# First layer of the compression MLP in decode: two products per half, or three over pairs of blocks

## What is computed

```
idx = arange(nc)[:, None] * 16 + arange(32)[None, :]
blk = rows[:, idx] + pos_emb          # blocks of 32 rows, one every 16 rows
hidden = gelu(blk @ w1)               # w1: (32 * 64) x 128
out = hidden @ w2                     # 128 x 64
```

## Time and profile before

| | us |
|---|---|
| median of 3 runs (lowest, highest) | 1865.72 (1865.47, 1865.9) |
| the profiled execution: its time | 1868.04 |
| the profiled execution: its span | 1866.3 |
| TensorE busy in the span | 1838.7 (99%) |
| TensorE weight loads | 1412.1 (76%) |
| VectorE busy | 1204.6 (65%) |
| ScalarE busy | 372.3 (20%) |
| GpSimd busy | 119.1 (6%) |
| mean granted TensorE clock | 0.998 |
| DMA | 199.86 MB, mean 107 GB/s |

### The profile page before, as it was taken

One profiled execution on the slowest core, in us unless ns is written; L12 is line 12 of the kernel. 1 busy time (PEld: TensorE's weight loads), 2 busy tenths in 40 slices (PEclk: granted clock), 3 DMA queues, 4 the chain that ended last, 5 costly groups with the idle time before them and its releaser, 6 DMA issues.

```text
span 1866.3 us, 27349 instructions
## 1 busy us (share of the span) xinstructions
PE 1838.7 (99%) x10438; PEld 1412.1 (76%) x10438; DVE 1204.6 (65%) x2676; ACT 372.3 (20%) x957; POOL 119.1 (6%) x218
## 2 busy tenths in 40 slices
PE   8999999999999999999999999999999999999999
PEld 7767777877777777777777676777777777777777
DVE  5899796442667677673268997954427667676631
ACT  2013375322100100000001134842211000100000
POOL 1011400110000000000000114001000000000000
PEclk9999999999999999999999999999999999999999
DMA  7302564663112222131242044057431212222111
GB/s 276 129 1 88 161 209 157 214 221 111 57 68 72 87 68 90 58 136 63 80 152 79 1 122 143 1 182 249 161 122 45 90 69 80 78 70 109 72 62 51
DMA packets 110390, 199.86 MB, mean 107 GB/s; under 512 B 13393, under 2 KB 81250, under 8 KB 105266
## 3 DMA queue, kind: packets, MB, share of 16 engines
q1 hardware_dynamic: 90946, 161.87, 25.5%
q0 software_dynamic: 5488, 29.93, 4.6%
q10 hardware_dynamic: 13824, 6.30, 1.3%
HBM read 190.36 MB, written 15.94 MB: 111 GB/s over the span
## 4 chain that ended last, share of the span: by engine, by line
PE 94%; DVE 4%; ACT 1%; issue 1%; DMA 0%; POOL 0%; DVEq 0%
PE ps L1065 30%; PE ps L1130 15%; PE ps L755 12%; PE ps L616 8%; PE ps L651 8%; PE ps L603 7%; PE ps L859 2%; PE ps L822 2%; PE ps L841 2%; PE ps L999 1%; PE ps L659 1%; PE ps L893 1%; PE ps L908 1%; PE ps L695 1%; PE ps L862 1%
## 5 line engine op out<-in xcount | busy, mean ns | idle before, releaser
L2140 DVE TENSOR_TENSOR xT<-xT,ps 128x288 f32<-128x288 f32 (+3 forms) x55 | 41.7, 758 | 153.2 <-PE ps L1130 152.9
L1065 PE MATMUL ps<-catT,rD 128*128 128x288 f32 x528 | 131.6, 406 | 0.0
L1065 PEld LDWEIGHTS ps<-catT,rD 128*128 128x128 f32 x528 | 100.3, 190 | 27.7
L1497 ACT ACTIVATE rD<-rD 128x592 f32<-128x592 f32 x44 | 30.7, 697 | 450.2 <-DVE rD L2082 450.2
L755 PE MATMUL ps<-WR,rD 128*128 128x254 f32 (+1 forms) x512 | 120.2, 382 | 0.2
L1065 PE MATMUL ps<-catT,XC 128*128 128x288 f32 x480 | 119.8, 406 | 0.4 <-DVE rD L2054 0.4
L1065 PE MATMUL ps<-rA,WR 128*128 128x288 f32 x448 | 117.8, 406 | 0.0
L1065 PEld LDWEIGHTS ps<-catT,XC 128*128 128x128 f32 x480 | 91.0, 190 | 26.2 <-issue 1.2
L755 PEld LDWEIGHTS ps<-WR,rD 128*128 128x128 f32 x512 | 93.0, 188 | 18.6 <-issue 2.9
L1065 PEld LDWEIGHTS ps<-rA,WR 128*128 128x128 f32 x448 | 85.1, 190 | 23.5
L616 PE MATMUL ps<-catT,WR 128*128 128x288 f32 x384 | 98.8, 410 | 2.0 <-ACT catT L1231 1.1
(11 more groups left out here) (376 smaller groups left out, 3317.7 us busy)
## 6 DMA issues: line engine op xcount, KB each, us to landing
WR<-in_w_up SPq DMA_DIRECT2D x56, 512.0 KB, 3.7
WR<-in_kvc SPq DMA_DIRECT2D x128, 128.0 KB, 2.3
rB<-in_w_up SPq DMA_DIRECT2D x32, 512.0 KB, 4.3
rD<-in_kvc SPq DMA_DIRECT2D x96, 128.0 KB
rD<-in_w_down SPq DMA_DIRECT2D x8, 1408.0 KB, 7.6
rB<-in_ksT SPq DMA_DIRECT2D x160, 64.0 KB, 4.0
rB<-in_w_down SPq DMA_DIRECT2D x6, 1408.0 KB, 6.0
WR<-in_w_glu SPq DMA_DIRECT2D x16, 512.0 KB, 3.9
```

Of the source, the lines that this page charges most:

```text
L1065: ins = mm(ps[:, bank, 0:HN], w[:, k, :], h[:, k, :], start=k == 0, stop=k == 3)
L2140: step(tt(x, x, src, ALU.add))
```

## The change

For two neighbouring blocks, 2m and 2m+1, the even one is A·r(2m) + B·r(2m+1) and the odd one A·r(2m+1) + B·r(2m+2). The change computes three products of half as many columns: first = B·r(2m), second = A·r(2m+1), third = (A+B)·(r(2m) + r(2m+1)). The even block is third − first − second, the odd one second(m) + first(m+1). This holds for the nine halves of passes 0 to 2 in both layers; the other jobs stay as they are.

- TensorE: `third(i, part, js)` does 8 products of 128 columns (64 chunks of 2 heads) for each of three parts, 24 for a half. Their order among the other work is new, and pass 0 to 2 put `third(1, 0)` ahead of pct.
- VectorE: `row_sums` adds the odd chunks onto the even ones in place (128x1024), once the first part has read them. `gelu_in_joined` joins the parts, reading copies in SBUF. `weight_sums_of` makes A+B at the end of the prompt, into the history part of XC, YB and `causal`.
- ScalarE: `thirds_kept` copies the bank to SBUF (256 and 128 columns); the tanh move behind these copies, and the key loads are issued seven, six and three instead of eight and eight.
- SP: the load of the next layer's convolution history moves from ahead of `fetch_cmp(5)` to behind the passes, and `causal` is loaded again there (layer 0 only).

```diff
@@ -251,6 +251,9 @@
...
+        kept = [rC[:, 8568:8824], rA[:, 4432:4560]]
+        wab = [[XC[:, c, XS0 + P * i:XS0 + P * (i + 1)] for c in range(CT) for i in range(2)],
+               [t[:, P * i:P * (i + 1)] for t in (YB, causal) for i in range(4)]]
...
@@ -301,6 +304,13 @@
...
+
+        def each_other(ap, at, m):
+
+            return bass.AP(ap.tensor, ap.offset + 2 * at, [list(ap.ap[0]), [4, m], [1, 2]])
+
+        def thirds(bank):
+            return [ps[:, bank, P * i:P * (i + 1)].rearrange("p (m h) -> p m h", h=2) for i in range(3)]
...
@@ -411,10 +421,6 @@
...
                 fetch_keys(l, 0)
-                sp.wait_ge(*count("conv_made", CT))
-                sp.wait_ge(*count("uc_out", 16))
-                if l + 1 < DEPTH:
-                    sp.dma_start(XC[:, :, XS0:XW], I["hist"][l + 1].rearrange("p (c n) -> p c n", c=CT)).then_inc(sh["hist_in"], 16)
                 sp.wait_ge(*count("hid_made", 2))
                 fetch_cmp(l, 5)
...
@@ -447,6 +453,10 @@
...
                         fetch_new(l, p + 2)
+                if l + 1 < DEPTH:
+                    sp.wait_ge(sh["hid_made"], 16 * (l + 1))
+                    sp.dma_start(XC[:, :, XS0:XW], I["hist"][l + 1].rearrange("p (c n) -> p c n", c=CT)).then_inc(sh["hist_in"], 16)
+                    sp.dma_start(causal[:, :], I["c_causal"]).then_inc(sh["causal_in"], 16)
                 down(l, 0)
...
@@ -925,10 +935,29 @@
...
-                    def half(i, js=range(16)):
+                    def third(i, part, js=range(NPAIR)):
+
                         job, b, n, c, bank = HALVES[p][i]
-                        earlier = [h for h in late if h[0] * 2 + h[2] < job * 2 + n and h[4] == bank]
-                        hidden(l, job, b, n, js=js, bank=bank, taken=2 * earlier[-1][0] + earlier[-1][2] + 1 if earlier else 6)
+                        if part == 0 and js[0] == 0:
+                            if n == 0:
+                                pe.wait_ge(*count(f"kv_in{rows_at(b)}", 256))
+                            if i == 2:
+                                pe.wait_ge(sh["hb_kept"], 9 * l + 3 * p + 1)
+                            elif p:
+                                pe.wait_ge(sh["hb_kept"], 9 * l + 3 * p - (0 if i == 0 else 1))
+                            elif i == 0:
+                                pe.wait_ge(sh["cmp_in"], 16 * l + 7)
+                        if part == 2 and js[0] == 0:
+                            pe.wait_ge(sh["hs_made"], 9 * l + 3 * p + i + 1)
+                            if p == 0:
+                                pe.wait_ge(sh["ab_made"], 2 * l + 2 - n)
+                        rows = kvc[rows_at(b)][:, 0:32 * PAST // CHUNK].rearrange("p (m q e) -> p q m e", q=2, e=32)[:, 1 if part == 1 else 0]
+                        for j in js:
+                            o = n * 16 + j * 2
+                            w = (w1[n][:, NPAIR + j, :], w1[n][:, j, :], wab[n][j])[part]
+                            ins = mm(thirds(bank)[part], w, rows[:, :, o:o + 2], start=j == 0, stop=j == NPAIR - 1)
+                        if js[-1] == NPAIR - 1 and part != 1:
+                            ins.then_inc(sh["hid_made" if part else "hb_made"], 1)
...
@@ -937,7 +966,10 @@
...
                     if more:
-                        half(0)
+                        third(0, 0)
+                        third(0, 1)
+                        pe.wait_ge(sh["cmp_max"], NPR * l + p + 1)
+                        third(1, 0)
...
@@ -953,8 +985,13 @@
...
                     if more:
-                        half(1)
-                        half(2, range(9) if p < 2 else range(16))
+                        third(0, 2)
+                        third(1, 1)
+                        third(1, 2)
+                        third(2, 0)
+                        if p == 2:
+                            third(2, 1)
+                            third(2, 2)
...
@@ -978,11 +1015,11 @@
...
                         keys_second(l, 2 * p + 3, NCS, sample_pick, CG[ca])
                         if p < 2:
-                            half(2, range(9, 11))
+                            third(2, 1)
                         else:
                             pe.wait_ge(*count("conv_done", 3))
                             pe.wait_ge(*count("wr_in0", 16))
-                            pe.wait_ge(sh["cmp_in"], 16 * (l + 1))
+                            pe.wait_ge(sh["hb_kept"], 9 * (l + 1))
                             first_left(0, 2)
...
@@ -1003,17 +1040,17 @@
...
                         if j == 5 and p < 2:
-                            half(2, range(11, 12))
+                            third(2, 2, range(1))
                         if j == 5 and p == 2:
                             first_left(2, 3)
                         if j == 11 and more:
                             if p < 2:
-                                half(2, range(12, 14))
...
                             keys_T(NCS)
                             if p < 2:
-                                half(2, range(14, 15))
+                                third(2, 2, range(3, 5))
                             keys_second(l, 2 * p + 4, NCS, sample_pick, CG[cb])
...
@@ -1025,7 +1062,7 @@
...
                         if p < 2:
-                            half(2, range(15, 16))
+                            third(2, 2, range(5, 8))
...
@@ -1413,6 +1450,14 @@
...
+                    def thirds_kept(i):
+                        act.wait_ge(sh["hid_made"], 16 * l + 8 + 3 * p + i)
+                        if 3 * p + i:
+                            act.wait_ge(sh["hx_made"], 9 * l + 3 * p + i)
+                        bank = HALVES[p][i][4]
+                        copy(kept[0], ps[:, bank, 0:2 * P])
+                        copy(kept[1], ps[:, bank, 2 * P:3 * P]).then_inc(sh["hb_kept"], 1)
...
@@ -1430,20 +1475,22 @@
...
                     if more:
-                        fetch_keys(range(8))
+                        fetch_keys(range(7))
...
                     if more:
-                        tanhed(tanh[0], NCS)
-                        fetch_keys(range(8, 16))
+                        thirds_kept(0)
+                        fetch_keys(range(7, 13))
                     act.wait_ge(*count("s_masked"))
...
                     if more:
-                        tanhed(tanh[1], NCS)
+                        tanhed(tanh[0], NCS)
+                        thirds_kept(1)
                         if p == 2:
-                            tanhed(tanh[2], NCS)
+                            tanhed(tanh[1], NCS)
+                            thirds_kept(2)
...
@@ -1455,6 +1502,8 @@
...
                         values_kept(NCS, Vc[ba % 4], 2)
+                        tanhed(tanh[1 if p < 2 else 2], NCS)
+                        fetch_keys(range(13, 16))
                         keys_kept(NCS, KcT[ba % 4])
...
@@ -1758,6 +1808,36 @@
...
+            def row_sums(b, n):
+
+                dve.wait_ge(*count("hb_made"))
+                rows = kvc[rows_at(b)][:, 0:32 * PAST // CHUNK].rearrange("p (m q e) -> p q m e", q=2, e=32)[:, :, :, 16 * n:16 * (n + 1)]
+                tt(rows[:, 0], rows[:, 0], rows[:, 1], ALU.add).then_inc(sh["hs_made"], 1)
+
+            def gelu_in_joined(n, s, bank):
+
+                dve.wait_ge(*count("hb_kept"))
+                count("hid_made")
+                first, second, third = [t.rearrange("p (m h) -> p m h", h=2) for t in (kept[0][:, 0:P], kept[0][:, P:2 * P], kept[1])]
+                even, odd = each_other(CX[s][n], 0, 64), each_other(CX[s][n], 1, 63)
+                step(tt(even, first, second, ALU.add))
+                stt(odd, second[:, 0:63], posb[:, n:n + 1], first[:, 1:64], ALU.add, ALU.add)
+                stt(even, third, posb[:, n:n + 1], even, ALU.add, ALU.subtract).then_inc(sh["hx_made"], 1)
+                dve.wait_ge(*count("hx_made"))
+                x, g = CX[s][n][:, 0:2 * NCS], CG[s][n][:, 0:2 * NCS]
+                step(stt(g, x, 0.044715, x, ALU.mult, ALU.mult))
+                stt(g, g, 1.0, x, ALU.add, ALU.mult).then_inc(sh["cmp_in"], 1)
+
+            def weight_sums_of(n):
+                if n:
+                    for t, i in ((YB, 0), (causal, 4)):
+                        ins = tt(t.rearrange("p (j m) -> p j m", j=4), w1[1][:, i:i + 4], w1[1][:, NPAIR + i:NPAIR + i + 4], ALU.add)
+                else:
+                    ins = tt(XC[:, :, XS0:XS0 + 2 * P].rearrange("p c (i m) -> p c i m", i=2),
+                             w1[0][:, 0:NPAIR].rearrange("p (c i) m -> p c i m", i=2),
+                             w1[0][:, NPAIR:2 * NPAIR].rearrange("p (c i) m -> p c i m", i=2), ALU.add)
+                ins.then_inc(sh["ab_made"], 1)
...
@@ -1854,6 +1934,8 @@
...
+                if l:
+                    dve.wait_ge(sh["causal_in"], 16 * l)
                 mask(0)
...
@@ -1885,6 +1967,9 @@
...
+                weight_sums_of(1)
+                dve.wait_ge(sh["uc_out"], 16 * (l + 1))
+                weight_sums_of(0)
```

(32 more changed lines are left out.)

## The result

| | us |
|---|---|
| before, median of 5 runs (lowest, highest) | 1865.9 (1865.47, 1867.39) |
| after, median of 5 runs (lowest, highest) | 1857.72 (1854.34, 1857.97) |
| after, the profiled execution: time, span | 1857.72, 1855.9 |
| after, mean granted TensorE clock | 0.994 (before 0.998) |

The ratio is 0.9948, with a 95% interval of 0.9936 to 0.9959. The kernel is faster, by 8.2 us. The forecast was 21.4 us, and its range (1836 to 1855) misses the result.

The account below looks back on a forecast made before the run. TensorE was taken to bound passes 0 to 2. A layer gains 14.8 - 0.2 - 1.5 - 2.5 = 10.6 us, two layers 21.2: 1868.0 becomes 1846.8, the median, 2.3 lower, 1844.5 us; range 1836 to 1855.

Parts of the forecast that it names:

- The products: Halves in passes 0 to 2: 48 records of 128 columns at 113 ns, 5.42 us a half, 1.56 less.
- the third and fourth rivals: Products: dear wider stride, 139 ns a record, about 1860 to 1864 (0.08); weight loads not hidden, 221 ns, 1931 (0.05).
- The row sum: VectorE, pass 0: a sum of 1024 elements takes 1.2 us, between 1.0 and 1.4.
- Pass 0: Shrinks to about 30.2 us; TensorE waits 0.2 us (nothing to 0.6) for the softmax's exponentials.
- Sequence 7's rows: Pass 1: SP's last page lands at +16.3 after pass 0's last product; third(2, 0) needs it at +14.8.
- The stall of 1.5 us: Pass 1, before third(2, 0): TensorE waits 1.5 us (0.5 to 2.5) for late rows.
- With 5.2 us to land: Pass 2: sequence 6's last page lands at +39.3, third(1, 0) needs it at +36.8; stall 2.5 us (0 to 4).
- the second rival: Waits cost twice as much: earlier gathers push pages out, lateness passes on; 8.4 us of stalls a layer, 1852.9; chance 0.22.
- Pass 1: Shrinks to about 30.3 us, with TensorE waiting for a DMA before third(2, 0).
- Other edits: at nothing, up to 1 us once: History and `causal` loads, two issues and under 1 MB in front of 439.45: nothing, up to 1 us once.

Follow-up runs that it names:

- gather_late: The kernel after, with GpSimd waiting for all of sequence 6's rows before gathering pass 2's values; 1846.67 us, and 1847.22 when measured again.
- busy_wait: The kernel after, with 18 unread products on constants filling TensorE's idle time ahead of third(1, 0) in pass 2; 1850.75 us.
- before_gather_late: Control: the kernel before, with pass 2's gathers waiting for sequence 6's rows; 1865.61 us, ratio 0.9997.
- one_gather_late: The kernel after, with only the second of pass 2's two gathers waiting for sequence 6's rows; 1848.87 us.
- late_and_split: The kernel after, with both gathers late and ScalarE's first seven key loads split, three ahead of the pct copy and four later; 1848.78 us.
- need_later: The kernel after, with pct, imp and third(0, 2) ahead of third(1, 0) in pass 2, other thirds reordered and one row sum later; 1852.69 us.

## Why the prediction was right and wrong

**Right.** The products. `third` has 16 records in 1.79 us, 112 ns (372.71 to 374.50 above; the forecast had 113), so the wide stride and the weight loads together cost at most 3 ns over the 109 of the bare columns, and the third and fourth rivals are out. The Trainium skill's rule (TensorE: Matmul & The Clock Gate, The mechanism) that a load overlaps products only for another row group would have given 1931; the trace disagrees. The row sum took 1.22 us (forecast 1.2). Pass 0, the one without late loads, was forecast at 29.0 us from 33.7 and has 28.8 and 29.4. Sequence 7's rows came as worked out, +16.3 in the forecast. The last two pages of layer 0, issued by 346.8, landed in 4.5 us, about 16 us after the end of pass 0's last product (335.2); `third(2, 0)` starts at 351.85, without a wait that shows:

```profile
WR<-in_kvc SPq DMA_DIRECT2D x2, 128.0 KB, 4.5
```

The stall of 1.5 us there was right in size but stands elsewhere: `imp` waits 1.55 us first, so TensorE is no longer early at `third(2, 0)`.

**Wrong, first step:** "With 5.2 us to land", for sequence 6's rows. I took the landing of a page from the earlier trace rows, in which no gather ran, though the same paragraph said that the gathers would start earlier. It also said that they ran beside half of the pages before; they started at 373.69, when SP had two or three pages left. The trace of before had the price of such company, at the start of pass 1: the gathers start at 340.0 and 341.3, and the pages issued from 342.5 to 344.5 us (columns as in the earlier trace rows) travel beside them:

```profile
WR<-in_kvc SPq DMA_DIRECT2D x4, 128.0 KB, 7.0
```

The last pages took 7.9 us; the stall was 4.9 and 5.5 us, not 2.5 (my bound was 4), 5.5 us too much in all. gather_late takes it away by moving the gathers alone. That is the mechanism of the second rival, "gathers that start earlier push the pages out"; it had 0.22 and 1852.9.

**Wrong, second step:** a step that is missing. Every stall was counted at its own length. After 4.9 and 5.5 us of idle time TensorE came back at half clock, 4.5 us in all by busy_wait's comparison. With it even the second rival, at 1852.9, was too fast.

**Smaller terms.** Pass 1 is 0.4 and 0.8 us longer than forecast: in layer 0 the exponentials add 0.15 before the transpositions, in layer 1 `imp` waits 1.9 and not 1.5. Pass 0 adds 0.2 over both layers; before its transpositions TensorE waits for nothing in layer 0 and 0.44 us in layer 1 (forecast 0.2). "Other edits: at nothing, up to 1 us once" was 1.7: outside the passes, against before_gather_late, 0.2 us stand ahead of the first pass, 0.6 between the layers and 0.9 behind the last pass 2 (of these 0.6 is a wait in pass 3, whose releaser isn't shown; busy_wait has neither the wait nor the 0.9). Which edit they belong to wasn't tried. The 0.6 between the layers needn't belong to any: the profile of before has as much more than before_gather_late there. In both after and before the clock falls in layer 1's prompt, where eight records of 384 columns behind a wait of 1.70 us take 2.93 us in after; behind the same wait they take 1.56 at full clock in before_gather_late and busy_wait.

The sum, over both layers: 5.5 (idle) + 4.5 (clock) + 1.2 (pass 1) + 0.2 (pass 0) + 1.7 (outside) = 13.1 us, and 1857.7 less 1844.5 is 13.2. In gather_late the first two are gone, and it measures 1846.7 and 1847.2, the lowest medians of the study; the intervals of one_gather_late and late_and_split overlap with its own.

## What to carry to other kernels

When a change makes one engine faster, list the transfers that it needs earlier and the ones that it triggers earlier, and price the landing of the first from a row in which the second run beside them: here a page took 2.1 to 2.2 us ahead of the gathers and 7.9 behind them. A transfer that nobody needs soon (here the gathers) can be told to wait for the urgent one; here nothing waited for the gathered values. And where a stall of several microseconds is forecast on TensorE, add what the clock may take afterwards: here stalls of 4.9 and 5.5 us cost another 2.6 and 1.9.

## What was not expected of the hardware

- The clock. After 4.92 us without a product the granted clock was 0.50 and stayed there for nearly 6 us of full work, so that 16 records took 3.75 us instead of 1.79. The Trainium skill (TensorE: Matmul & The Clock Gate, HAM oscillation — how this bites in real kernels) tells of such waits for a DMA after which the engine comes back at the slow clock; this trace agrees, and it was a rule to weigh before. Shorter waits did it too: need_later has 2.31 us of idle time before `imp` in pass 1 of layer 1, with the windows below behind it, while 2.7 us in pass 2 of the same layer left the clock at 1.00. At the same place one_gather_late came back at 0.60 (1260 to 1264 us) after 1.83 us, and after stayed at 1.00 with 1.94. So the length of a wait of 1.8 to 2.7 us doesn't tell; what does stays open.

```profile
1262.00:1264.00 2.00, 1.59 (x7) 1.59 (x8) 0.82 (x5) 0.77 (x2) 0.00 (x0) 0.59 1.02 306
1264.00:1266.00 2.00, 2.00 (x12) 2.00 (x11) 1.86 (x8) 0.00 (x0) 0.00 (x0) 0.55 0.96 317
```

- The landing of the last pages, 128 KB each: 3.5 us with no gather beside them, 7.9 with 2 MB.
- Four of the kernels with thirds scatter more from run to run (4.3 to 6.7 us) than before (2.3 to 4.0 us on the same chips); busy_wait has only 1.4. The mean granted clock goes with it: the fastest and the slowest run of late_and_split have 1845.18 us at 0.999 and 1851.86 at 0.995, those of gather_late 1844.42 at 0.998 and 1850.06 at 0.996. Why the clock of one kernel differs between executions wasn't settled. Differences of a few microseconds between these kernels can be clock alone.
